# A reordered opening: x first, quartered first weights, x statistics spread between low parts, a Sqrt for the norm, ropes ahead of the gate bounds

## What is computed

```python
for l in range(DEPTH):
    h = rmsnorm(x, norm_g[l])
    proj = h @ w_in[l]
    (a_q, a_k, a_v, a_gate, b_u, b_v, b_gate, c_q, c_f, c_i, c_gate, merge) = jnp.split(proj, SPLIT_IDX, axis=-1)
    qa = rope(a_q.reshape(b_, s_, A_HEADS, A_HEAD_DIM), positions)
    ka = rope(a_k.reshape(b_, s_, A_KV_HEADS, A_HEAD_DIM), positions)
    out_a = sliding_window_attention(qa, ka, va, attn_sinks[l]) * jax.nn.silu(a_gate)
    ...
    f = lb + (1.0 - lb) * jax.nn.sigmoid(fr)      # lb: the gate bounds, from hgrn_lb
    ...
    x = x + y
return rmsnorm(x, final_g)
```

## Time and profile before

| | us |
|---|---|
| median of 3 runs | 1040.75 (1040.24 to 1041.43) |
| the profiled execution's own time | 1040.38 |
| its span, first to last instruction | 1038.5 |
| PE busy | 1015.2 (98%) |
| DVE, ACT, POOL busy | 641.0, 517.5, 287.1 |

### The profile page before, as it was taken

How to read it: one execution, slowest core, us unless ns; L and a number is a source line. 1 busy time by engine, 2 the same in 40 slices (tenths; PEclk the granted TensorE clock), 3 DMA queues, 4 the chain that set the end, 5 groups by cost and what they waited for, 6 DMA issues and landing times.

```text
span 1038.5 us, 15307 instructions
## 1 busy us (share of the span) xinstructions
PE 1015.2 (98%) x6388; PEld 856.0 (82%) x6388; DVE 641.0 (62%) x838; ACT 517.5 (50%) x804; POOL 287.1 (28%) x144
## 2 busy tenths in 40 slices
PE   7789999999999999999999999999999999999997
PEld 6669899888888888888888889988888888888876
DVE  5786884899645445355547779479983353444552
ACT  5846665675462323232447667477656333332333
POOL 1111111542422314143212111163243232323420
PEclk9889999999999999999999999999999999999999
DMA  6422222212223232333243222122231232323602
GB/s 217 133 81 66 74 67 82 81 45 79 82 65 118 81 102 87 96 102 122 88 136 112 82 82 82 42 82 82 81 102 62 81 102 81 102 81 102 198 5 81
DMA packets 93412, 94.71 MB, mean 91 GB/s; under 512 B 2256, under 2 KB 91552, under 8 KB 93344
## 3 DMA queue, kind: packets, MB, share of 16 engines
q1 hardware_dynamic: 93216, 93.70, 29.0%
q10 hardware_dynamic: 128, 0.04, 0.0%
HBM read 91.64 MB, written 2.10 MB: 90 GB/s over the span
## 4 chain that ended last, share of the span: by engine, by line
PE 93%; DVE 3%; ACT 2%; issue 1%; DMA 1%; SPq 0%; DVEq 0%; ACTq 0%
PE pj L500 27%; PE pj L502 26%; PE pj L501 26%; PE mx L635 2%; PE mx L500 1%; PE mx L501 1%; PE mx L502 1%; PE mx L575 1%; PE mx L598 1%; PE mx L695 1%; ACT w_hi L810 1%; PE mx L663 1%; PE mx L583 1%; PE mx L673 1%; DVE w_lo L1256 1%
## 5 line engine op out<-in xcount | busy, mean ns | idle before, releaser
L1146 POOL TENSOR_TENSOR w_lo<-w_raw,w_hi 128x1024 fp32r<-128x1024 f32 (+1 forms) x89 | 195.5, 2197 | 579.8 <-ACT w_hi L810 579.5
L500 PE MATMUL pj<-h_hi,w_hi 128*128 128x512 f32 x832 | 330.3, 397 | 0.0
L502 PE MATMUL pj<-h_hi,w_lo 128*128 128x512 f32 x832 | 324.6, 390 | 0.0
L501 PE MATMUL pj<-h_lo,w_hi 128*128 128x512 f32 x832 | 324.5, 390 | 0.0
L810 ACT ACTIVATE w_hi<-w_raw 128x1024 fp32r<-128x1024 f32 (+1 forms) x180 | 160.1, 939 | 162.6 <-PE pj L502 162.5
L1256 DVE TENSOR_TENSOR w_lo<-w_raw,w_hi 128x1024 fp32r<-128x1024 f32 (+1 forms) x91 | 165.2, 1815 | 74.1 <-ACT w_hi L810 73.8
L500 PEld LDWEIGHTS pj<-h_hi,w_hi 128*128 128x128 f32 x832 | 156.8, 188 | 34.4 <-issue 2.6
L502 PEld LDWEIGHTS pj<-h_hi,w_lo 128*128 128x128 f32 x832 | 156.5, 188 | 33.1
L501 PEld LDWEIGHTS pj<-h_lo,w_hi 128*128 128x128 f32 x832 | 156.7, 188 | 32.2 <-issue 1.0
L1353 DVE TENSOR_TENSOR merge_gate<-pj,rstd 128x512 f32<-128x512 f32 x48 | 33.2, 692 | 162.9 <-PE pj L502 162.9
L920 ACT ACTIVATE merge_gate<-merge_gate,small 128x512 f32<-128x512 f32 x48 | 34.3, 715 | 89.3 <-DVE merge_gate L1353 89.3
(11 more groups left out here) (255 smaller groups left out, 1494.7 us busy)
## 6 DMA issues: line engine op xcount, KB each, us to landing
w_raw<-in_w_in SPq DMA_DIRECT2D x61, 1024.0 KB, 5.5
w_raw<-in_w_branch SPq DMA_DIRECT2D x24, 512.0 KB, 3.4
w_raw<-in_w_out SPq DMA_DIRECT2D x6, 1024.0 KB, 5.1
x_tokens<-in_x SPq DMA_DIRECT2D x4, 512.0 KB, 7.2
w_raw_last<-in_w_out SPq DMA_DIRECT2D x2, 1024.0 KB, 7.3
w_raw<-in_w_in SPq DMA_DIRECT2D x2, 512.0 KB, 6.2
sp_w_rows<-in_sp_w SPq DMA_DIRECT2D x2, 512.0 KB, 5.5
out<-out_low SPq DMA_DIRECT2D x4, 256.0 KB, 2.0
```

What stands on the lines that cost most here:

```text
L500: pe.matmul(bank, wh, ah, start=first, stop=False)
L501: pe.matmul(bank, wh, al, start=False, stop=False)
L502: return pe.matmul(bank, wl, ah, start=False, stop=final)
L1146: return pool.tensor_tensor(out=dst, in0=full, in1=hi.bitcast(f32), op=ALU.subtract)
```

## The change

- **Transfers.** The constants move from SP's queue to the head of ScalarE's. SP's order was constants, x0, w 0 to 3, x1, w 4 to 7, x2, x3; it is now x0, w 0-1, x1, w 2-3, x2, w 4 to 7, x3 (w k to k': row blocks of unit 0).
- **First weights in quarters.** `quarter(q)` splits two row blocks at a time on ScalarE and VectorE; PE waits for the first quarter at k = 0 and for the second at k = 2.
- **Small transposes.** The transpose of the vector rows (L471) stands on PE between x0's and x1's; VectorE copies its result ahead of the first low part.
- **x statistics.** The eight `bn_stats` are spread between the low parts, and the norm's sum now comes before unit 1's low half and before the angles.
- **Root.** ScalarE's Ln and Exp become one Sqrt, followed by a reciprocal on VectorE.
- **Hand-written steps.** The diagonal product moves from after job 3 to after job 2. On ScalarE the root goes to step 0, `rstd_row` and then the sines to step 2, the bounds' Exp to step 6, the swap of the keys from step 6 to 4. On VectorE the diagonal and then the angles go to step 0, and `bounds` from step 5, between two ropes, to step 7, behind all ropes.

```diff
-            sp.dma_start(CST[:, :], consts[:, :]).then_inc(cst_in, 16)
             load_x(0)
-            sp.dma_start(buf[:, 0:4, :], src[:, 0:4, :]).then_inc(first_half, 16)
+            sp.dma_start(buf[:, 0:2, :], src[:, 0:2, :]).then_inc(first_in[0], 16)
             load_x(1)
+            sp.dma_start(buf[:, 2:4, :], src[:, 2:4, :]).then_inc(first_in[1], 16)
+            load_x(2)
             sp.dma_start(buf[:, 4:8, :], src[:, 4:8, :]).then_inc(raw_in[0], 16)
-            load_x(2)
             load_x(3)
...
-            for k in range(4):
-                transpose_x(k)
+            transpose_x(0)
+            transpose_x(1)
             pe.wait_ge(vec_in, 16 * 3)
             pe.transpose(PJ[2][:, 0:64], VR[0:64, :], CST[0:64, 0:64]).then_inc(vecT_done, 1)
             pe.wait_ge(p_norm, 1)
+            transpose_x(2)
+            transpose_x(3)
...
-                    if n == 3 and layer == 0:
+                    if n == 2 and layer == 0:
+                        pe.wait_ge(xT_evac, KT)
                         pe.wait_ge(fill_done, 1)
                         pe.wait_ge(p_diag, 1)
...
+            act.dma_start(CST[:, :], consts[:, :]).then_inc(cst_in, 16)
...
             first_h(0)
+            quarter(0)
             first_h(1)
-            act.wait_ge(first_half, 16)
-            split_half(0, 0)
             first_h(2)
+            quarter(1)
             first_h(3)
...
-                    chained(act.activation(RT, MS, ACT.Ln, bias=EP, scale=1.0))
-                    act.activation(RT, RT, ACT.Exp, scale=-0.5).then_inc(p_rstd, 1)
+                    act.activation(MS, MS, ACT.Sqrt, bias=EP, scale=1.0).then_inc(p_root, 1)
...
-                    phase[0].append((first_sines,))
-                    phase[2].append((first_rstd,))
-                    phase[2].append((bounds_exp,))
-                    phase[3].append((rstd_row,))
+                    phase[0].append((first_rstd,))
+                    phase[2].append((rstd_row,))
+                    phase[2].append((first_sines,))
+                    phase[6].append((bounds_exp,))
...
             def rstd_diagonal():
+                dve.wait_ge(p_root, 1)
+                dve.reciprocal(RT, MS).then_inc(p_rstd, 1)
                 dve.wait_ge(p_rstd, 1)
...
+                    phase[0].append((rstd_diagonal,))
+                    phase[0].append((angle_first,))
+                    phase[0].append((angle_rest,))
                     phase[2].append((trig,))
-                    phase[2].append((rstd_diagonal,))
-                    phase[5].append((bounds,))
+                    phase[7].append((bounds,))
```

More of the change, by code:

```diff
@@ L284, in build @@
         norm_in, vec_in, cst_in, pos_in = sem("norm_in"), sem("vec_in"), sem("cst_in"), sem("pos_in")
-        first_half = sem("first_half")
+        first_in = [sem(f"first_in{q}") for q in range(2)]
+        quarter_hi, quarter_lo = sem("quarter_hi"), sem("quarter_lo")
         fill_done, xT_done, xT_evac = sem("fill_done"), sem("xT_done"), sem("xT_evac")
@@ L290, in build @@
         p_bounds = sem("p_bounds")
-        p_ms, p_rstd, p_diag = sem("p_ms"), sem("p_rstd"), sem("p_diag")
+        p_ms, p_root, p_rstd, p_diag = sem("p_ms"), sem("p_root"), sem("p_rstd"), sem("p_diag")
         vecT_done, p_diff, p_exp, p_trig, p_sin = sem("vecT_done"), sem("p_diff"), sem("p_exp"), sem("p_trig"), sem("p_sin")
@@ L490, in claim @@
                     u, t = JOBS[n]
-                    if t == 0:
+                    if t == 0 and layer * NU + u == 0:
+                        pe.wait_ge(quarter_lo, 1)
+                    elif t == 0:
                         pe.wait_ge(w_lo, layer * NU + u + 1)
-                        if layer * NU + u > 0:
-                            pe.wait_ge(w_lo_vec, layer * NU + u + 1)
+                        pe.wait_ge(w_lo_vec, layer * NU + u + 1)
                     if n >= NJP + 2:
@@ L514, in project_both @@
                                 transpose_x(2 * k + 1)
+                            if k == KT // 4:
+                                pe.wait_ge(w_lo, 1)
                             if k == KT // 2:
@@ L833, in _, with quarter @@
             act.wait_ge(p_norm, 1)
+            def quarter(q):
+                act.wait_ge(first_in[q], 16)
+                k = slice(2 * q, 2 * q + 2)
+                buf = raw_of(0).rearrange("p (k c) -> p k c", c=UC)
+                out_ = WHI[:, 0, :].rearrange("p (k c) -> p k c", c=UC)
+                act.activation(out_[:, k, :], buf[:, k, :], ACT.Copy).then_inc(w_hi if q else quarter_hi, 1)
             first_h(0)
+            quarter(0)
             first_h(1)
-            act.wait_ge(first_half, 16)
-            split_half(0, 0)
             first_h(2)
+            quarter(1)
             first_h(3)
@@ L843, in _ @@
             split_half(0, 1)
+            first_h(4)
+            first_h(5)
             x_evac(2)
             x_evac(3)
[L846 to L847 removed]
             first_h(6)
@@ L1260, in split_lo, with quarter, x_stats @@
                 split_half(v, 1)
+            def quarter(q):
+                dve.wait_ge(w_hi if q else quarter_hi, 1)
+                k = slice(2 * q, 2 * q + 2)
+                raw, hi, lo = (a.rearrange("p (k c) -> p k c", c=UC)[:, k, :]
+                               for a in (raw_of(0), WHI[:, 0, :], WLO[:, 0, :]))
+                dve.tensor_tensor(out=lo, in0=raw, in1=hi.bitcast(f32), op=ALU.subtract)\
+                   .then_inc(w_lo if q else quarter_lo, 1)
+            def x_stats(half, tb):
+                return dve.bn_stats(XS[:, tb, half, :], XTOK[:, tb, half * T:(half + 1) * T])
             dve.wait_ge(normT_done, 1)
@@ L1274, in _ @@
             dve.tensor_copy(LBT[:, 24:32], PJ[2][:, 56:64]).then_inc(p_vec, 1)
+            first_low(0)
+            quarter(0)
+            first_low(1)
+            first_low(2)
+            quarter(1)
+            first_low(3)
+            dve.wait_ge(x_in[0], 16)
+            dve.wait_ge(x_in[1], 16)
+            x_stats(0, 0)
+            x_stats(0, 1)
             split_half(0, 1)
@@ L1277, in _ @@
             first_low(5)
-            angle_first()
+            x_stats(0, 2)
+            x_stats(0, 3)
             first_low(6)
             first_low(7)
-            split_lo(1)
-            angle_rest()
-            for j in range(KT // 2):
-                dve.wait_ge(x_in[j], 16)
+            dve.wait_ge(x_in[2], 16)
+            dve.wait_ge(x_in[3], 16)
             for tb in range(TB):
-                for half in range(2):
-                    last = dve.bn_stats(XS[:, tb, half, :], XTOK[:, tb, half * T:(half + 1) * T])
+                last = x_stats(1, tb)
             pchain(last)
```

9 lines of the change are left out of this document (3 added, 6 removed).

## The result

| | changed kernel | kernel before |
|---|---|---|
| median of 8 runs | 1032.19 us (1031.4 to 1034.06) | 1036.3 us (1035.19 to 1041.43) |
| profiled execution, span | 1032.96, 1031.1 | 1040.38, 1038.5 |
| ratio | 0.9946 [0.9926, 0.9965] | |

The change makes the kernel faster, but the profiled execution is 7.4 us shorter, not 11.3. The kernel before has two levels: three of its runs lie at 1040.2 to 1041.4, five at 1035.2 to 1036.6. The runs shown ahead of the prediction and its trace were all of the upper one. Against the five runs of the lower level (median 1035.67) the change wins about 3.5 us. Each ratio, the one in the table too, is to comparison runs of the kernel before at both levels, so medians are the better measure of a difference between two experiments; the changed kernel has 1032.19 here and 1031.97 in a second series.

What follows compares the result with a forecast made beforehand. PE, busy 1015.2 of 1038.5 us, bounds the kernel, so only its idle and slow stretches can be won: 0.5 + 5.6 + 1.6 + 2.4 + 1.2 = 11.3 off 1040.38, plus 0.37 for the median, gives 1029.4 us; range 1026.3 to 1033.3.

Steps and rivals of the forecast that it cites:

- rival 2: PE's wait ahead of the scores is at least 3.5 us and the clock falls; 1032.1 to 1033.0 us, chance 0.14.
- Start, 0.5: Opening: x1 lands earlier, first product at 9.7 and job 2 at 24.7; 0.5 us won, between 0 and 1.0.
- First wait, 5.6: PE's wait for `rstd_diagonal`: gone, as `p_diag` is ready at 25.9, 4.2 us ahead of PE; 5.6 us won.
- its slow clock, 1.6: PE's slow stretch after the wait for `rstd_diagonal` (diagonal product, value transposes, job 4's first matmul) goes; 1.6 us won.
- Rival 4: Job 2 waits for unit 1's `w_lo`; 1 to 2 us more give 1030.4 to 1031.4, chance 0.10.
- Second wait, 2.4: PE's wait for the last rotated query, ahead of the scores: 1.9 to 2.0 us instead of 4.4; 2.4 us won.
- Clock after it, 1.2: PE's slow clock after the wait ahead of the scores: 1.2 us won, between 0 if it falls and 2.0 if not.
- Bounds behind the ropes at nothing: `bounds` delays the scores' maximum by 2 us, hidden under jobs 8 and 9: costs nothing; 2 without that cover.
- Rival 3: The sines, ahead of the ropes, are late by a table load, 1.28 us; gain 8.8, 1031.9 us, chance 0.04.
- Rival 1: No wait ahead of the scores, if GpSimd's pieces miss the angles or fourth rope; gain 14.1, 1026.7 us, chance 0.13.
- Rival 5: Small transfers served late in the opening, start slips: at most 3.4 us, 1032.8; chance 0.03 slower, 0.04 landing at 9 to 11.

Runs made afterwards that it cites:

- the best kernel: The changed kernel with unit 4's low half directly behind the fifth rope, value copies behind that, and bounds behind the first maximum of the scores: 1026.74 us.

## Why the prediction was right or wrong, point by point

The forecast was 1029.4 and the range 1026.3 to 1033.3; 1032.19 lies in the range and outside the forecast's own 1028.4 to 1031.2. **What happened is rival 2**, the second wait stays long and the clock falls, which gave 1032.1 to 1033.0 and had a chance of 0.14. The range holds because that rival is in it, not because the main line of the forecast was right.

- **Start, 0.5.** In the profiled execution 0.4, over six traces each 0.9, by medians 1.3: right in sign; the size lies between 0.4 and 1.3 and is no closer known. "First product at 9.7" was wrong (10.15). PE begins with the norm rows, which now stand second on ScalarE's queue and arrive at 5.72, so x's first transposes began at 5.91 instead of 5.61; from there PE ran without a gap, through the vector rows' transpose too, to the first product. The prediction had written that the delay of ScalarE's row loads costs nothing, because ScalarE is idle; it had not asked whether PE waits for those rows. The gain is larger than forecast where the fast pace comes earlier, which was the term's upper bound.
- **First wait, 5.6, and its slow clock, 1.6.** Right. `p_diag` was ready at 26.2 (forecast 25.9), PE asked at 30.39 (30.2), the clock is 1.00 from 36 to 46. Rival 4 did not occur in this trace, in which `w_lo` was done at 24.71 and job 2 began at 24.86; where the fast pace came early, in the kernel with the norm rows first, job 2 waited 0.2 for `w_lo`, so the margin is as small as forecast.
- **Second wait, 2.4: the step that failed.** It measured -0.3. The prediction's ropes' chain ended "the fifth to 60.7". That is the sum of work without the hold-up by GpSimd's half of unit 5, for which both rows stood in the earlier trace rows (68.49 and 68.10) and had even been read, as evidence for another stall. By its own numbers GpSimd would start at 58.9 + 1.2 = 60.1 (1.2 is also the distance in before's rows, 66.9 to 68.10), against a last operation of the rope from 60.0: a race, not a margin. The chain was besides 1.0 too short: the fourth rope ended at 57.1 (56.2), unit 4's low half at 59.1 (58.0). With that 1.0 the operation fell behind GpSimd's start and became 2.0 longer: 1.9 + 1.0 + 2.0, less 0.2 by which PE itself was later, is the 4.7. The kernels with the ropes earlier show the step in its place: wait 0.9 to 1.0.
- **Clock after it, 1.2.** Nothing, since the wait was 4.7. With a wait of 0.9 or 1.0 the clock did not fall. Near the 2.0 us of the forecast both ends that it named occur: behind the wait of 2.2 for the probabilities the clock stayed in one kernel and fell in the next.
- **Bounds behind the ropes at nothing.** True of the changed kernel, where the scores come late. With the scores where the forecast had them the cover of jobs 8 and 9 is too thin: a wait of 2.2, which moving the bounds once more took away.
- **The sum against 1040.38.** The profiled execution was of before's upper level. Against it the change wins 7.4, against the lower level about 3.5. The second level could not be read from three runs, all of the upper one; but the 0.39 us between two rows on which it hangs were in the trace.
- **Rival 3.** The sine followed its load of 1.28 at once (33.55 and 34.85), 1.30 behind it. The drain of another 1380 ns that the Trainium skill gives (page "ScalarE: Activation LUTs", "What ACT_TABLE_LOAD costs") is again not seen. **Rival 1** came out by another way: without a long second wait it gave 1026.7, and the best kernel, which keeps 0.9 of it, has 1026.74. That these agree to 0.1 is partly luck: the kernel has three edits more, and its opening was 1.1 earlier than in the changed kernel's first trace. **Rival 5** happened in small: the norm rows were late, and the vector rows, in time in the first trace (7.97), held PE 0.4 in the kernel with the ropes ahead of the copies.

The Trainium skill, page "SBUF — State Buffer", "Who interferes with whom", says that VectorE and GpSimd contend for a shared pair of ports and that the order of issue, not the shape of the operation, decides who is blocked. The traces agree: by 0.4 to 0.7 us of starting after GpSimd the same operation takes 2.7 instead of 0.69. The point above on the second wait is worked out from these rows.

## What to carry to other kernels

Where a slow engine's work holds up a faster one, list for the new schedule every piece of the slow engine, what releases it, and which operation it will land on; then put there one that nobody waits for. The gain of removing one wait is known only when the next meeting point has been worked out with all its hold-ups, and the cover of whatever was moved behind it. Three runs of a kernel can all lie at one of two levels; two rows of its trace that meet within half a microsecond are the warning.

## What the runs showed of the hardware

- While GpSimd works on its half of a unit (2.4 to 3.1 us), VectorE stands still also in some operations that read one tensor: 8 columns took 2.36 to 2.37 instead of 0.17, a copy 2.41 to 2.43 instead of 0.36. That covers more than the two-operand work of which the prediction spoke. It does not cover all: under GpSimd's half from 20.95 to 23.36 in the changed kernel, four `bn_stats` took 0.62 each and four `bn_aggr` 0.42 together, as without it, and only the product of 4 columns behind them was held to the end of GpSimd's row (0.45 instead of 0.16). An operation of VectorE that already ran was not held up, but GpSimd's was then longer: 2.99 with `w_lo` running for its first 0.7, 2.41 where VectorE was idle at its start (43.19).
- In the opening, nine matmuls of the changed kernel started every 0.43 us, the same step as at 66.31 to 68.02, where the granted clock is 0.50. The windows print 1.00 for both that stretch and what follows, but the trace has no record of the clock ahead of 13.99; the first one, 1.00, stands there, and at 11.38 in the second execution. The fast pace began at 14.08 and at 11.62.
- How long after PE's stop the clock fell was not the same each time: 2.0 and 2.2 us in the kernel before, but 5.3 at the first wait of its second trace; 2.6 in the changed kernel, and 4.6 in its second execution, as the wait ended (0.58 in the window 62.5 to 63); 4.2 and 5.1 at the waits of 7.8. Waits of 0.9 and 1.0 left it at 1.00, waits of 2.2 did so in one trace and not in another.
